# The mixer's norm taken behind its first GEMM, its weights' stream ahead of the constants' rows

## What is computed

```python
def rms_norm(x, w):
    y = x * rsqrt(mean(x * x, axis=-1) + 1e-6)
    return y * w

h = rms_norm(x, norm_mix_w)               # 256 x 2048
proj = h @ w_in                           # 2048 x 7680
u_s5, x_lru, y_lru = proj[:, :512], proj[:, 512:2048], proj[:, 2048:3584]
gates = sigmoid(proj[:, 3584:] + b_gate)  # 2 x 2048 columns
# later: gelu(y_lru), a causal convolution and a scan over x_lru, an S5 scan over u_s5
```

## Time and profile before

| | us |
|---|---|
| median of three runs | 2768.43 |
| the profiled execution | 2762.75 |
| its span | 2761.0 |
| busy in it: TensorE, VectorE, ScalarE | 2581.2, 1306.5, 933.8 |
| first product of the first GEMM | 23.85 from the span's start |
| first product of the block of code behind it | 193.62 |

### The profile page before, as it was taken

One profiled execution on the slowest core, in us unless ns is written; L12 is line 12 of the kernel. 1 busy time (PEld: TensorE's weight loads), 2 busy tenths in 40 slices (PEclk: granted clock), 3 DMA queues, 4 the chain that ended last, 5 costly groups with the idle time before them and its releaser, 6 DMA issues. The chain is left out here.

```text
span 2761.0 us, 37500 instructions
## 1 busy us (share of the span) xinstructions
PE 2581.2 (93%) x14098; PEld 1715.4 (62%) x14098; DVE 1306.5 (47%) x2533; ACT 933.8 (34%) x1666; POOL 109.6 (4%) x117
## 2 busy tenths in 40 slices
PE   8999999999888889999998999999899989998999
PEld 7984555887444444447974775865456855774557
DVE  5654693665411112325764554563535543553435
ACT  5545121444221212224532433432224422431224
POOL 0001111020011110010000000000002000000000
PEclk9999999999999999999999999999999999999999
DMA  7754343454399999993443013543334542432232
GB/s 301 223 206 158 132 152 137 179 197 166 114 423 422 422 422 422 403 393 138 177 160 114 33 48 108 197 172 118 107 140 152 196 170 83 170 140 104 76 107 92
DMA packets 80308, 529.62 MB, mean 192 GB/s; under 512 B 9088, under 2 KB 13568, under 8 KB 18848
## 3 DMA queue, kind: packets, MB, share of 16 engines
q1 hardware_dynamic: 76128, 514.50, 49.1%
q0 software_dynamic: 3456, 11.02, 1.6%
q10 hardware_dynamic: 576, 2.10, 0.2%
HBM read 520.24 MB, written 7.34 MB: 191 GB/s over the span
## 5 line engine op out<-in xcount | busy, mean ns | idle before, releaser
L397 DVE TENSOR_TENSOR split_wl<-ring,split_wh 128x512 fp32r<-128x512 f32 x416 | 290.2, 708 | 193.0 <-ACT split_wh L369 191.1
L369 ACT ACTIVATE split_wh<-ring 128x512 fp32r<-128x512 f32 x416 | 260.2, 631 | 253.0 <-PE ps L343 253.0
L341 PE MATMUL ps<-split_wh,split_xh 128*128 128x512 f32 x832 | 326.1, 392 | 0.6 <-DVE split_wl L397 0.6
L342 PE MATMUL ps<-split_wl,split_xh 128*128 128x512 f32 x832 | 325.0, 391 | 0.0
L651 PE MATMUL ps<-ring,xT 128*128 128x512 f32 x640 | 289.5, 605 | 31.0 <-issue 8.0
L2152 PE MATMUL ps<-ring,yT 128*64 128x256 f32 x2048 | 247.8, 386 | 52.9 <-DMA ring<-in_weights 48.8
L454 PE MATMUL ps<-features_xh,features_wh 128*128 128x256 f32 x832 | 236.9, 285 | 1.5 <-DVE features_wl L445 1.5
L456 PE MATMUL ps<-features_xh,features_wl 128*128 128x256 f32 x832 | 235.3, 283 | 0.0
L2152 PEld LDWEIGHTS ps<-ring,yT 128*64 128x64 f32 x2048 | 137.5, 137 | 156.2 <-DMA ring<-in_weights 91.9
L651 PEld LDWEIGHTS ps<-ring,xT 128*128 128x128 f32 x640 | 120.4, 193 | 177.1 <-issue 163.0
L651 PE MATMUL ps<-ring,yT 128*128 128x512 f32 x448 | 205.9, 611 | 21.7 <-issue 11.4
(11 more groups left out here) (650 smaller groups left out, 3648.2 us busy)
## 6 DMA issues: line engine op xcount, KB each, us to landing
ring<-in_weights SPq DMA_DIRECT2D x468, 1024.0 KB, 5.0
x_res<-in_x SPq DMA_DIRECT2D x1, 2048.0 KB, 7.5
yT<-in_mem SPq DMA_DIRECT2D x1, 2048.0 KB, 15.8
rel_skew<-lru_feat POOLq DMA_DIRECT2D x1, 2048.0 KB, 50.0
mem_features<-yT ACTq DMA_DIRECT2D x4, 512.0 KB, 6.6
s_wb<-in_s_bc POOLq DMA_DIRECT2D x4, 512.0 KB, 4.0
s_wc<-in_s_bc POOLq DMA_DIRECT2D x4, 512.0 KB, 4.1
gate_bias<-in_gate_bias POOLq DMA_DIRECT2D x8, 256.0 KB, 4.0
```

What stands on the lines that cost most here:

```text
L341: nc.tensor.matmul(out, xh[:, kc, at], wh[:, c % deep, :], start=kc == 0, stop=False)
L342: nc.tensor.matmul(out, xh[:, kc, at], wl[:, c % deep, :], start=False, stop=False)
L369: nc.scalar.activation(wh[:, c % deep, :], raw(unit, turn, c), ACT.Copy).then_inc(w_high.sem, 1)
L397: last = nc.vector.tensor_tensor(wl[:, c % deep, :], raw(unit, turn, c), wh[:, c % deep, :], ALU.subtract)
```

## The change

The norm's block of code goes. Its class `LateNorm` works inside the first GEMM's block of code: raw `x` is turned in 32 transposes into all eight PSUM banks, the gain is applied as it is taken out, and the GEMM runs on that. The sum of squares is made in four half pieces on ScalarE, placed around the first unit and behind the second and third; mean, root and reciprocal follow. A token's reciprocal root is put on a diagonal, multiplied by ones on TensorE and copied, so that it stands in every partition along the tokens (`row`). Each block's result is multiplied by that row as VectorE takes it from PSUM, and the gates' results by the same number as a per-partition scale in `take`. In `setup` four weight units are issued ahead of the constants' rows, SyncE's wait goes, and TensorE gets eight products of ones.

```diff
+class LateNorm:
+    def transpose(self, pe):
+        pe.wait_ge(k.first_loaded, 48)
+        for g in range(self.GROUPS):          # 8 groups, 4 transposes each, bank g
+            ...
+            last.then_inc(tr.sem, 1)
+    def evict_act(self, act, n):              # waits tr.at(2 * n); 2 x (128x256, scale = gain); drain
+    def evict_dve(self, dve, n):              # waits tr.at(2 * n + 1); the same on VectorE; drain
+    def piece_there(self, act, n):            # n > 0: waits for VectorE's eviction n - 1
+    def squares(self, act, t, m):             # Square of 128x1024 with accumulation; drain
+    def mean(self, dve):                      # waits for all four squares; add, drain, scale
+    def root(self, act):                      # Sqrt of 128x2
+    def spread(self, dve):                    # reciprocal, drain, 2 x (ident * rstd, 128x128)
+    def make_row(self, pe, bank):             # waits for spread; 2 products ones x diagonal, 128 columns
+    def copy_row(self, dve, bank):            # waits for make_row; 128x256 from PSUM; drain
+    def row_copied(self, pe):                 # waits for copy_row
 gemm_features, tensor:
-                keep_busy(k, pe, 7, 5)
+                norm.transpose(pe)
+                norm.banks_free(pe)           # evictions 0 and 1 of both engines
                 for b in range(blocks):
+                    if b == 1:
+                        norm.row_copied(pe)
...
                         split.multiply(pe, 4 * (b % 2), kc)
+                        if b == 0 and kc == KC - 1:
+                            norm.make_row(pe, 4)
 gemm_features, scalar:
                             if b == 0 and g * UNIT_KC + c in split.STARTS:
-                                split.x_high(act, split.STARTS.index(g * UNIT_KC + c))
+                                n = split.STARTS.index(g * UNIT_KC + c)
+                                if n == 0:
+                                    act.wait_ge(k.first_loaded, 48)
+                                    norm.squares(act, 0, 0)
+                                    norm.evict_act(act, 0)
+                                elif n + 1 < norm.GROUPS // 2:
+                                    norm.evict_act(act, n + 1)
+                                norm.piece_there(act, n)
+                                split.x_high(act, n)
+                                if n == 0:
+                                    norm.evict_act(act, 1)
+                                    norm.squares(act, 0, 1)
...
+                        if b == 0 and 1 <= g <= 2:
+                            norm.squares(act, 1, g - 1)
+                        if b == 0 and g == 3:
+                            norm.root(act)
 gemm_features, vector:
+                                (evict_dve 0 ahead of x_low 0, 1 behind it, 2 and 3 ahead of x_low 1 and 2)
+                        if b == 0 and g == 2:
+                            norm.mean(dve)
+                        if b == 0 and g == 3:
+                            norm.spread(dve)
+                            norm.copy_row(dve, 4)
...
+                dve.wait_ge(k.skewed, 16)
                 finish(blocks - 1)
 setup:
+            stream(k, sp, RING // 2)
             load(k, sp, k.rows[:, :], k.dram["rows"].to_broadcast([P, ROW_N]))
             stream(k, sp, RING)
-            sp.wait_ge(k.first_loaded, 48)
 setup, tensor, behind the credits:
+            pe.wait_ge(k.ones_made, 1)
+            for _ in range(8):
+                nc.tensor.matmul(k.ps[:, 7, 0:P], k.ones[:, :], k.ones[:, :], start=True, stop=True)
 mixer:
-    norm_to_features(k, "norm_mix", early=8)
 mixer_in, finish of a block b:
     def finish_act(act, b, j):
         if b < 4:
-            return nc.scalar.activation(place(b, 0), pairs(j, 0), ACT.Copy)
-        nc.scalar.activation(place(b, 0), pairs(j, 0), ACT.Gelu_apprx_tanh)
-        return nc.scalar.activation(place(b, 1), pairs(j, 1), ACT.Gelu_apprx_tanh)
+            return act.drain()
+        act.wait_ge(evac_v.sem, evac_v.at(b))
+        return nc.scalar.activation(place(b), place(b), ACT.Gelu_apprx_tanh)
     def finish_dve(dve, b, j):
-        if b < 4:
-            return nc.vector.tensor_copy(place(b, 1), pairs(j, 1))
         if b == 4:
-            return nc.vector.memset(feat[:, 0:LRU_HEADS, 0:PAD], 0.0)
-        return nc.vector.drain()
+            nc.vector.memset(feat[:, 0:LRU_HEADS, 0:PAD], 0.0)
+        return nc.vector.tensor_tensor(place(b), k.ps[:, 4 * j:4 * j + 4, 0:SEQ], bc(norm.row[:, :], 1, UNIT_KC), ALU.mult)
 GateProduct.take:
-        k.nc.scalar.activation(self.out(b), k.ps[:, 6:8, :], ACT.Copy).then_inc(taken.sem, 1)
+        for t in range(NT):
+            last = k.nc.scalar.activation(self.out(b)[:, t, :], k.ps[:, 6 + t, :], ACT.Copy, scale=self.rstd[:, t:t + 1])
+        last.then_inc(taken.sem, 1)
```

More of the change, by code:

```diff
@@ L459, in multiply, with __init__, banks_free, ended @@
         last.then_inc(self.k.ev("w_used").sem, 1)
-def gemm_features(k, x, blocks, finish_act, finish_dve, mem, rel, prm, decay):
+class LateNorm:
+    GROUPS = KC // 2
+    def __init__(self, k, scope, gain):
+        self.k, self.gain = k, gain
+        self.st = k.sb(scope, "late_stat", [P, 12])
+        self.row = k.sb(scope, "late_row", [P, SEQ])
+        self.diagonal = k.sb(scope, "late_diagonal", [P, NT, P])
+        self.junk = k.yT[:, KC:KC + 4, :].rearrange("p a b -> p (a b)")
+        self.rstd = self.st[:, 10:12]
+    def transpose(self, pe):
+        k, tr = self.k, self.k.ev("tr")
+        pe.wait_ge(k.first_loaded, 48)
+        for g in range(self.GROUPS):
+            for c in range(2):
+                for t in range(NT):
+                    at, f = c * SEQ + t * P, (2 * g + c) * P
+                    last = k.nc.tensor.transpose(k.ps[:, g, at:at + P], k.x[:, t, f:f + P], k.ident[:, :])
+            last.then_inc(tr.sem, 1)
+    def banks_free(self, pe):
+        act_a, dve_a = self.k.ev("act_a"), self.k.ev("dve_a")
+        pe.wait_ge(act_a.sem, act_a.at(1))
+        pe.wait_ge(dve_a.sem, dve_a.at(1))
+    def evict_act(self, act, n):
+        k, tr = self.k, self.k.ev("tr")
+        act.wait_ge(tr.sem, tr.at(2 * n))
+        for c in range(2):
+            kc = 4 * n + c
+            k.nc.scalar.activation(k.xT[:, kc, :], k.ps[:, 2 * n, c * SEQ:(c + 1) * SEQ], ACT.Copy, scale=k.col(self.gain, kc))
+        act.drain().then_inc(k.ev("act_a").sem, 1)
+    def evict_dve(self, dve, n):
+        k, tr = self.k, self.k.ev("tr")
+        dve.wait_ge(tr.sem, tr.at(2 * n + 1))
+        for c in range(2):
+            kc = 4 * n + 2 + c
+            k.nc.vector.tensor_scalar(k.xT[:, kc, :], k.ps[:, 2 * n + 1, c * SEQ:(c + 1) * SEQ], k.col(self.gain, kc), None, ALU.mult)
+        dve.drain().then_inc(k.ev("dve_a").sem, 1)
+    def piece_there(self, act, n):
+        dve_a = self.k.ev("dve_a")
+        if n:
+            act.wait_ge(dve_a.sem, dve_a.at(n - 1))
+    def squares(self, act, t, m):
+        k, ssq = self.k, self.k.ev("ssq")
+        k.nc.scalar.activation(self.junk, k.x[:, t, m * (D // 2):(m + 1) * (D // 2)], ACT.Square,
+                               accum_out=self.st[:, 2 * t + m:2 * t + m + 1])
+        act.drain().then_inc(ssq.sem, 1)
+    def mean(self, dve):
+        nc, st, ssq, ms = self.k.nc, self.st, self.k.ev("ssq"), self.k.ev("ms")
+        dve.wait_ge(ssq.sem, ssq.at(3))
+        sums = st[:, 0:4].rearrange("p (t a) -> p t a", t=NT)
+        nc.vector.tensor_tensor(st[:, 4:6], sums[:, :, 0], sums[:, :, 1], ALU.add)
+        dve.drain()
+        nc.vector.tensor_scalar(st[:, 6:8], st[:, 4:6], 1.0 / D, EPS, ALU.mult, ALU.add).then_inc(ms.sem, 1)
+    def root(self, act):
+        ms, root = self.k.ev("ms"), self.k.ev("root")
+        act.wait_ge(ms.sem, ms.at(0))
+        self.k.nc.scalar.activation(self.st[:, 8:10], self.st[:, 6:8], ACT.Sqrt).then_inc(root.sem, 1)
+    def spread(self, dve):
+        nc, root, scaled = self.k.nc, self.k.ev("root"), self.k.ev("scaled")
+        dve.wait_ge(root.sem, root.at(0))
+        nc.vector.reciprocal(self.rstd, self.st[:, 8:10])
+        dve.drain()
+        for t in range(NT):
+            last = nc.vector.tensor_scalar(self.diagonal[:, t, :], self.k.ident[:, :], self.rstd[:, t:t + 1], None, ALU.mult)
+        last.then_inc(scaled.sem, 1)
+    def make_row(self, pe, bank):
+        k, scaled = self.k, self.k.ev("scaled")
+        pe.wait_ge(scaled.sem, scaled.at(0))
+        for t in range(NT):
+            last = k.nc.tensor.matmul(k.ps[:, bank, t * P:(t + 1) * P], k.ones[:, :], self.diagonal[:, t, :], start=True, stop=True)
+        last.then_inc(k.ev("small_mm").sem, 1)
+    def copy_row(self, dve, bank):
+        k, mm = self.k, self.k.ev("small_mm")
+        dve.wait_ge(mm.sem, mm.at(0))
+        k.nc.vector.tensor_copy(self.row[:, :], k.ps[:, bank, 0:SEQ])
+        dve.drain().then_inc(k.ev("stacked").sem, 1)
+    def row_copied(self, pe):
+        stacked = self.k.ev("stacked")
+        pe.wait_ge(stacked.sem, stacked.at(0))
```

(56 more changed lines are left out.)

## The result

| | median us | lowest to highest | runs |
|---|---|---|---|
| before | 2766.40 | 2762.84 to 2771.39 | 20 |
| changed | 2772.53 | 2768.16 to 2777.73 | 20 |

The ratio of the two is 1.0026, with a 95% interval of 1.0019 to 1.0033: 7.2 us slower (5 to 9); the medians lie 6.1 apart. I had forecast 1.05 us slower, within what can be told from no change. The sign was right, the size was not. In the profiled execution of the changed kernel the span is 2770.4 us.

The account below looks back on a forecast made before the run. TensorE was taken to bound the first GEMM, the norm what precedes it. The terms, 3.95 - 1.2 - 1.9 - 0.5 - 1.3 - 0.1, gave 1.05 us slower: 2769.5 us, range 2765.5 to 2773.5.

Parts of the forecast that it names:

- Setup's end: Opening, eight products of ones behind TensorE's credits: the block of code ends at 13.8 us, bounds 12.3 to 14.1.
- my bound for all slow: Opening: setup's end at 14.1 us if all passes of ones run at the slow clock.
- From there to the first product: Front, ScalarE's order decides: 6.1 us, bounds 5.9 to 6.9, first product at 19.9, gain 3.95 against 23.85.
- Step 1: First GEMM, block 0: TensorE waits 1.2 us for the second piece of weights, bounds 0.6 to 2.0.
- rival (2): Front: the clock falls while TensorE stands still, 1.7 us lost, 2.75 slower in sum, 2771.2; chance 0.14.
- The row: Between blocks 0 and 1: VectorE's row copy delays weights, TensorE begins block 1 1.9 us late, 1.3 to 2.4.
- Block 4: Step 4 of block 4: VectorE's longer product instead of a copy delays TensorE 0.5 us, bounds 0 to 0.6.
- Block 5: ScalarE's table load passes in its wait for VectorE: cost 0, or 0.9 us if it comes behind.
- The last block: First GEMM's end: VectorE's product, then ScalarE's Gelu, nothing beside them, cost 1.3 us, bounds 0.9 to 1.6.
- The gates' copy: LRU branch's end: two operations of 0.59 us replace one of 1.02, cost 0.1 us, bounds 0 to 0.3.
- The streams: Loads of weights and memory in changed order: either order lands in time, cost 0.
- the upper bound of 5.5 us: Whole sum with all bounds at the slow side: 5.5 us slower.

Follow-up runs that it names:

- the kernel with its ends mended: Changed kernel plus a two-element Gelu ahead of ScalarE's wait in block 5 and the last block's result taken out in two halves: ratio 1.0013 to before.

## Why the prediction was right and wrong, step by step

- **Setup's end, 13.8 forecast:** 14.2. Right in kind, and the step on which the sign hung. The passes of ones are 0.213 apart as I had them, but the clock doesn't rise within them, the first is 0.13 longer and the last ends 0.42 behind its start: my bound for all slow, 14.1.
- **From there to the first product, 6.1:** 6.2. Gain 3.4 in place of 3.95.
- **Step 1, 1.2:** 1.1 where the clock stays up (22.99 - 20.45 - 1.44 in the kernel with its ends mended). Where it falls, it takes up part of the wait, as rival (2) had it.
- **The row, 1.9:** 2.03. Right.
- **Block 4, 0.5:** 0.4. Right. **Block 5, 0:** 0.5. The load came behind the wait, the case that I had priced at 0.9 and not taken; I had read its order from a case where nothing had to be waited for.
- **The last block, 1.3:** 1.3, right.
- **The gates' copy, 0.1:** 0.5. Mis-sized twice: a copy with a per-partition scale takes 0.68, not the 0.59 of the earlier trace rows, and a second place, at 437 us, waits for one.
- **The streams, 0:** nothing in any trace waits for a weight unit there. Right.

Two slips in the sum as recorded change nothing above: the next block of code belonged at 194.6, since the gates' 0.1 comes after it, and the upper bound of 5.5 us ends at 2773.9, not 2773.5.

The waits first. In the two profiles whose front has ones and shows no fall, and whose edits leave the stage alone (195.65 and 195.83), the next block of code is 2.0 and 2.2 us late; with the gates' 0.5 that is 2.5 to 2.7 at 440 us. So 1.5 of the missing 6 us are terms that I had too small: block 5, the gates, setup's end.

The step that failed is the price of stillness on TensorE: rival (2), the clock's fall, which I gave 14 in 100, and the ends of the two stages, which I summed as wait alone (1.3 and 0.1 us) with nothing for the clock. I took one place (the front) and held that 2.6 us of stillness was too short. The runs show falls behind 2.5, 2.97 and even 1.9 us of it, in the front and in two more places, both ahead of a stretch in which TensorE is nearly always busy. With the frequencies seen in the profiles that is 4/6 x 0.65 + 4/6 x 1.7 + 3/8 x 1.7 = 2.2 us in the mean (an estimate). Over all executions it is more: 11 to 14 us more at half the clock, 4 to 5 us by the estimate above. With the 2.5 to 2.7 of the waits that makes 6.5 to 7.6, against 7.2 measured twice. And with the three places filled, where the time at half is no longer than before's, the kernel is 2.7 us slower by the medians and 3.6 by the ratio: about its waits. The sign was right for the reason given, the waits; but that it could be measured at all is the clock's doing, since 2.6 us alone lie within the 0.2% that I called no change.

By the Trainium skill ("TensorE: Matmul & The Clock Gate", Part 1: The HAM clock gate) idle time returns the slow clock and activity lifts it. The traces agree: passes 0.12 us apart become 0.21 apart behind the 2.54 us of stillness, and the transposes behind the ones are 0.11 apart. The same section cautions that the count of slow products varies from run to run; here whether the clock falls at a place varies too, in four of six profiles and not in the others.

What stays open is where the rest of the half-clock time lies. The falls seen at the three places hold about 6 of the 11 to 14 us. Falls further on (720 to 760 us, around 2640) are more frequent in the unfilled changed kernel's profiles than in before's. At 720 to 760 us the waits of TensorE are the same, 2.7 and 4.0 us. Why filling three places takes away nearly all of the added time at half isn't shown either.

## What to carry to other kernels

Whatever is queued behind the last work of the last engine of a stage that ends by a barrier costs all engines its full length; find that engine first (the wait of the others at the barrier names it) and lighten it before removing any other wait. A small operation that has to pass from one engine to another and back belongs a step ahead of its use, not at the point where the producer's loop ends. A wait on the product engine is to be priced as wait plus the chance that the clock falls over it, times what the next products cost at half speed; a few idle products in a wait that exists anyway cost nothing measurable here. And where every execution has its mean clock on record, compare that first: it says over all of them what single profiles can't.

## What was new about the hardware

- The clock fell behind stillness of 1.9 to 3 us, in some executions and not in others, and up to 1 us after work had begun again (still from 192.65 to 195.65, down from about 196.6 in the kernel with only its front filled). One such fall cost 1.7 us at the stage's end.
- The mean granted clock was 0.9873 and 0.9877 over 20 and 11 executions with the change and 0.9897 over 34 without: 11 to 14 us more at half the clock, and none more than before's (58 us against 60) once three waits were filled with small products.
- ScalarE's copy of 128x512 from PSUM with a per-partition scale takes 0.68 us, and two take 1.26; one of 128x1024 without takes 1.02.
- ScalarE's table load stood behind a wait on another engine's result (148.52 us), and ahead of it once a small operation of the same function was placed there.
